# A two-layer decoder step on one core: first rows in a buffer of their own, decode rows kept in place, value products in pairs

## What is computed

```python
def trunk_layer(x, pos, conv_buf, shift_prev, rwkv_state, mem_k, mem_v, attend, p):
    h = rms_norm(x, p['pre_g'])
    proj = jnp.einsum('bsd,de->bse', h, p['w_in'])
    ...
    o_lat = attend(q_lat, q_rope, ckv, krope)
    ...
    x = x + rms_norm(jnp.einsum('bse,ed->bsd', mixed, p['w_out']), p['post_g'])

for l in range(DEPTH):                      # DEPTH = 2
    mk, mv = mem_kv(mem_prompt, mem_norm_g[l], w_mem_k[l], w_mem_v[l])
    xp, ... = trunk_layer(xp, pos_p, ..., mk, mv, prompt_attend, p)   # 2048 prompt rows
    xs, ... = trunk_layer(xs, pos_s, ..., cache_mem_k[l], cache_mem_v[l], ..., p)   # 8 decode rows
```

## Time and profile before

| | |
|---|---|
| median of 3 runs | 3659.76 us (3657.32 to 3660.7) |
| the profiled execution | 3655.21 us, its span 3653.4 us |
| TensorE busy, products | 3548.5 us, 97% of the span |
| TensorE, loads of weights (beside the products) | 2609.2 us, 71% |
| VectorE busy | 1693.9 us, 46% |
| ScalarE busy | 1385.9 us, 38% |
| GpSimd busy | 163.4 us, 4% |
| TensorE's granted clock, mean | 0.996 of full |
| moved by DMA | 411.45 MB, 113 GB/s |

### The profile page before, as it was taken

One profiled execution on the slowest core, in us unless ns is written; L12 is line 12 of the kernel. 1 busy time (PEld: TensorE's weight loads), 2 busy tenths in 40 slices (PEclk: granted clock), 3 DMA queues, 4 the chain that ended last, 5 costly groups with the idle time before them and its releaser, 6 DMA issues.

```text
span 3653.4 us, 74825 instructions
## 1 busy us (share of the span) xinstructions
PE 3548.5 (97%) x30920; PEld 2609.2 (71%) x30920; DVE 1693.9 (46%) x4364; ACT 1385.9 (38%) x3767; POOL 163.4 (4%) x284
## 2 busy tenths in 40 slices
PE   7999999999999999999989999999999999999998
PEld 5768686776768777686567686868777687776864
DVE  2535454454545535445325354544535454353553
ACT  2333434243343433534423333343433434335343
POOL 1000000000000000000000000000000000000000
PEclk9999999999999999999999999999999999999999
DMA  5343343425224143232343434334153241532411
GB/s 177 92 151 107 131 129 111 140 68 168 86 101 146 49 167 98 83 123 67 100 140 95 160 94 151 100 121 135 61 182 95 97 129 48 176 95 77 135 55 65
DMA packets 316661, 411.45 MB, mean 113 GB/s; under 512 B 26509, under 2 KB 276315, under 8 KB 316323
## 3 DMA queue, kind: packets, MB, share of 16 engines
q1 hardware_dynamic: 294243, 358.88, 30.5%
q0 software_dynamic: 11648, 41.95, 3.3%
q10 hardware_dynamic: 10432, 5.84, 0.6%
HBM read 384.84 MB, written 21.80 MB: 111 GB/s over the span
## 4 chain that ended last, share of the span: by engine, by line
PE 90%; ACT 5%; issue 2%; DVE 2%; ACTq 1%; DVEq 0%; DMA 0%; SPq 0%; POOL 0%; POOLq 0%
PE bank L714 82%; PE bank L718 8%; ACT hT L2141 1%; ACT Q L2301 1%; ACTq L2280 0%; ACT L2281 0%; ACT PT L2417 0%; ACT qr L2300 0%; DVEq L1393 0%; ACT Sm L2374 0%; ACT Q L2299 0%; DVE bon L1523 0%; ACT Bp L2322 0%; ACT T L2279 0%; ACT PT L2225 0%
## 5 line engine op out<-in xcount | busy, mean ns | idle before, releaser
L714 PE MATMUL bank<-hT,win 128*128 128x256 f32 (+3 forms) x7168 | 1607.5, 379 | 4.5 <-ACT hT L2141 4.5
L714 PEld LDWEIGHTS bank<-hT,win 128*128 128x128 f32 (+1 forms) x7168 | 1259.8, 186 | 222.4 <-issue 40.7
L714 PE MATMUL bank<-kv,Q 96*128 96x512 f32 (+3 forms) x640 | 276.5, 529 | 0.2
L1698 DVE TENSOR_REDUCE ml<-bank 128x1 f32<-128x512 f32 (+3 forms) x320 | 195.4, 611 | 158.8 <-PE bank L714 148.4
L718 PEld LDWEIGHTS bank<-cst,Sm 128*128 128x128 f32 x1344 | 153.5, 140 | 123.7 <-issue 67.6
L718 PE MATMUL bank<-cst,Sm 128*128 128x128 f32 x1344 | 213.7, 280 | 17.9 <-ACT Sm L2374 9.8
L2374 ACT ACTIVATE Sm<-bank,ml 128x512 f32<-128x512 f32 (+3 forms) x320 | 199.9, 625 | 74.4 <-DVE ml L1703 68.6
L714 PE MATMUL bank<-wout,mix 128*128 128x512 f32 x480 | 217.9, 600 | 6.8 <-ACT hT L2141 6.5
L2163 ACT ACTIVATE mix<-bank 128x256 f32<-128x256 f32 x128 | 49.0, 383 | 318.4 <-PE bank L714 318.4
L714 PEld LDWEIGHTS bank<-wout,mix 128*128 128x128 f32 x480 | 88.7, 191 | 113.1 <-issue 112.2
L2270 ACT ACTIVATE mix<-bank 128x512 f32<-128x512 f32 (+1 forms) x68 | 39.6, 596 | 250.2 <-PE bank L714 250.2
(11 more groups left out here) (480 smaller groups left out, 5691.2 us busy)
## 6 DMA issues: line engine op xcount, KB each, us to landing
win<-in_w_in SPq DMA_DIRECT2D x176, 1024.0 KB, 5.3
wout<-in_w_out SPq DMA_DIRECT2D x60, 512.0 KB, 7.7
out_xres<-xin SPq DMA_DIRECT2D x16, 1024.0 KB
xin<-in_x_prompt SPq DMA_DIRECT2D x15, 1024.0 KB
xin<-out_xres SPq DMA_DIRECT2D x15, 1024.0 KB
win<-in_w_in SPq DMA_DIRECT2D x16, 896.0 KB, 4.9
PT<-in_w_out SPq DMA_DIRECT2D x28, 512.0 KB, 3.6
XX<-in_w_out SPq DMA_DIRECT2D x28, 512.0 KB, 4.1
```

Of the source, the lines that this page charges most:

```text
L714: return pe.matmul(out, lhsT, rhs, start=start, stop=stop, skip_group_check=True)
L1698: v.tensor_reduce(top, bank[:, 0:w], AX, MAX)
```

## The change

Three things are changed.

1. The rows of block 0 get a buffer of their own, `xfirst`, in `kv[:, 4096:6144]`. SP loads it behind the memory weights (in layer 1 after a wait for the stored rows of block 0 of layer 0); ScalarE's load is gone. TensorE turns the first tile right behind the memory products, into banks 4 and 5, and ScalarE takes it and normalises the second tile before `memory_out`.
2. In layer 1 the decode rows are taken from `xin` as the residual left them. SP raises the count of `s_x` where it issued the load.
3. In the attention two value groups are issued together at every fourth chunk, in place of one at every second.

```diff
+        xfirst = kv[:, 4096:6144].rearrange("p (j d) -> p j d", j=2)
...
+        s_xf = sig("first_rows", 16)
...
# sync, memory_loads(l), at its end
+                if l:
+                    sp.wait_ge(s_od.h, s_od.at((l - 1) * IT + 1, 0))
+                sp.dma_start(xfirst, prompt_rows(l, 0)).then_inc(s_xf.h, 16)
...
                     sp.wait_ge(s_xn.h, s_xn.at(px, 0))
+                    if px == l * IT + 2:
+                        sp.sem_inc(s_x.h, 16)
                     sp.dma_start(xin[:, :, :], prompt_rows(l, tok)).then_inc(s_x.h, 16)
...
-                sp.dma_start(xin[0:NS, 0, :], sample_rows(l)).then_inc(s_x.h, 16)
+                    sp.dma_start(xin[0:NS, 0, :], sample_rows(l)).then_inc(s_x.h, 16)
+                else:
+                    sp.sem_inc(s_x.h, 16)
...
# tensor, attention
-                    if c >= m + 2 and (c - m) % 2 == 0:
+                    if c > m and (c - m) % 4 == 0:
+                        values((c - m) // 2 - 2)
                         values((c - m) // 2 - 1)
-                for x in range((n - m - 1) // 2, n // 2):
+                for x in range((n - m - 1) // 4 * 2, n // 2):
                     values(x)
...
# tensor, start of a layer, behind the memory products
                         turn_x(l * IT, 0, 2)
+                turn_x(l * IT + 1, 0, bank=4)
                 pe.wait_ge(s_mem["kvr"].h, s_mem["kvr"].at(l, 1))
...
-                pe.wait_ge(s_hT.h, s_hT.at(l * IT, 2))
-                turn_x(l * IT + 1, 0)
                 pe.wait_ge(s_wr.h, s_wr.at(l, 1))
                 turn_x(l * IT + 1, 1)
...
# scalar
+                def rows_of(px):
+                    return xfirst if px == l * IT + 1 else xin
...
-                    act.wait_ge(s_x.h, s_x.at(px, 16))
+                    if px == l * IT + 1:
+                        act.wait_ge(s_xf.h, s_xf.at(l, 16))
+                    else:
+                        act.wait_ge(s_x.h, s_x.at(px, 16))
...
                 act.wait_ge(s_xn.h, s_xn.at(px, 2))
-                act.dma_start(xin[:, :, :], prompt_rows(l, 0)).then_inc(s_x.h, 16)
                 sum_squares(px + 1, 2, junk)
                 act.wait_ge(s_xt.h, s_xt.at(px, 2))
                 normalise(px + 1, 0)
-                act.wait_ge(s_mem["kv"].h, s_mem["kv"].at(l, 2))
                 take_h(px, 0, slice(T, T + NS), 2)
+                take_h(px + 1, 0, tile_cols(0), bank=4)
+                normalise(px + 1, 1)
                 memory_out()
-                take_h(px + 1, 0, tile_cols(0))
-                normalise(px + 1, 1)
                 take_h(px + 1, 1, tile_cols(1))
```

More of the change, by code:

```diff
@@ L2125, in sum_squares @@
                             act.drain()
-                        act.activation(out[:, 0:D], xin[:, j, :], ACT.Square, accum_out=st[:, j:j + 1]).then_inc(s_ss.h, 2 // tiles)
+                        act.activation(out[:, 0:D], rows_of(px)[:, j, :], ACT.Square, accum_out=st[:, j:j + 1]).then_inc(s_ss.h, 2 // tiles)
                     act.drain()
@@ L2133, in normalise @@
                     act.wait_ge(s_xr.h, s_xr.at(px, j + k))
-                    act.mul(xn[:, :], xin[:, j, :], st[:, 4 + j:5 + j]).then_inc(s_xn.h, k)
+                    act.mul(xn[:, :], rows_of(px)[:, j, :], st[:, 4 + j:5 + j]).then_inc(s_xn.h, k)
                 def take_h(px, j, cols, k=1, bank=6):
```

## The result

| | kernel before | changed kernel |
|---|---|---|
| median, beside each other on one chip | 3659.52 us (3657.32 to 3660.7) | 3637.95 us (3634.6 to 3639.97) |
| profiled execution, its span | 3655.21, 3653.4 us | 3639.97, 3638.2 us |
| mean granted clock in it | 0.996 | 0.994 |

What follows compares the result with a forecast made beforehand. TensorE, busy 97% of the span, was taken as the bound. From 3655.2 us, 9.2 for the layer starts and 12.1 for pairing left 3633.9 for the profiled execution, 3638.5 for the median; range 3627 to 3650.

Steps and rivals of the forecast that it cites:

- Part 3: Attention: issuing value groups in pairs saves 12.1 us over both layers, the ceiling of 19.7 less added waits.
- the ceiling: Attention: 68 value groups no longer stand apart, each saving 0.29 us for going in and out, 19.7 us.
- The loss: Last five turns of a block: ScalarE paces bare turns, so waits take back part of the saving, 7.6 us.
- Rival A: Attention: pairing gives nothing, as the 0.29 falls on engines' waits everywhere; 3650.6 us, chance 0.09.
- rival D: Attention: doubled value groups starve the row maxima, TensorE waits at each of the 68; 3690.7 us, chance 0.05.
- Part 1: Start of layer 0: turning the first tile earlier brings the second turn 3.01 us forward, plus 0.26; sum 3.3 us.
- 0.26 more, with a shorter gap ahead of it: Start of layer 0: the second turn, 1.30 us before, runs at its full-clock 1.04, gaining 0.26 us.
- Rival C: Start of layer 0: the load put ahead on SP isn't hidden, and layer 0 starts later; 3645 us, chance 0.06.
- Part 2: Start of layer 1: 3.0 from the same order, 0.9 from the second turn, 1.95 from the dropped decode-row load; 5.9 us.
- the second turn should take 1.04: Start of layer 1: the second turn falls from 1.94 to 1.04 us, 0.9 gained.
- 1.2 of that wait remain: Start of layer 1: TensorE's wait of 3.11 us for the normalised decode rows shrinks to 1.2.
- Rivals B and E: B: ceiling reached and clock stays up, 3626.6 us, chance 0.08. E: clock alone, 4.3 less, 3634, chance 0.12.

Runs made afterwards that it cites:

- with the clock held: Kernels given transposes nobody reads in TensorE's waits: the kernel before took 3647.6 us, with both starts changed 3636.94, the changed kernel 3625.21.
- tail_filled: Changed kernel with paired value groups only while score products are still issued, single groups behind the last five turns of a block; 3633.06 us, ratio 0.9928.
- start_only: Changed kernel with the pairing of value groups undone, so only the layer starts are changed; 3649.06 us, ratio 0.9974.
- in_place_only: Kernel before with only the decode rows left in place in layer 1, not stored and loaded again; 3657.41 us, ratio 0.9999.
- warm_before: Kernel before with transposes nobody reads put into TensorE's waits, 28 in place of 11 ahead of the second turn; 3647.6 us.
- warm: `tail_filled` with 182 transposes of the identity, which nobody reads, ahead of or behind TensorE's waits in six places; 3618.84 us, ratio 0.9897.
- own_buffer_only: Changed kernel, but layer 1 stores and loads the decode rows again as before; 3642.72 us, ratio 0.9961.
- split_pairs: Changed kernel with the score product put between the two value groups of a pair; 3654.48 us, ratio 0.9992.

## Why the prediction was right, point by point

**Part 3, a forecast of 12.1: the size and the mechanism right, its two terms each too large.** 11.9 by the windows, 11.7 with the clock held. That a passage costs busy time, and that bare turns at a block's end take part of it back, is what the runs show. But the ceiling of 68 x 0.29 = 19.7 was in fact 16.7 of busy time, since the 0.29, read in mid-block, doesn't hold for all 68 (0.25 on average, and 0.09 for the groups that `tail_filled` sets apart again). The loss was counted at 7.6, and TensorE's idle time in these stretches rose by 4.8. Both errors are about 3 us and cancel, which is luck. In blocks 0 and 1 likewise: 0.43 and 0.87 came for 0.58 and 0.58, and most of it is waiting that went, not passages. The forecast used one number for two blocks; the two differ by up to 0.6, and the sum of each pair agrees to 0.2. The forecast of 2.86 us from score to turn was for 16 pairs of products; what stands there above has 14, for which the same terms give 2.64. Rival A (nothing, 3650.6) falls by that, and rival D (row maxima starved) since no turn in mid-block waits that did not before.

**Part 1, a forecast of 3.3 for layer 0: the position right, one term wrong.** Block 0 starts 3.58 us earlier (49.08 for 52.66). The total is close, two of its parts aren't. Ahead of the decode tile's turn (32.13 for 33.40) lie 1.27, mostly because the memory products happened to take 8.80 us for 9.93, where 7.03 is full clock. From there to the second turn are 2.99, forecast at 3.01. Behind it 0.68 were lost. The term "0.26 more, with a shorter gap ahead of it" failed: after a wait of 1.27, shorter than the 3.39 before, the turn took 1.97, not 1.04. With the clock held the moved turn is worth 2.98. Rival C falls: the decode tile's turn starts before 33.4. Its normalised rows are there at 28.75 (26.98 before), 1.8 us later and not 3.5, well inside the cover.

**Part 2, a forecast of 5.9 (3.0 + 0.9 + 1.95): 4.78 in the changed kernel, 5.66 in `start_only`.** By positions in the changed kernel the chain of the decode rows gave 1.82, for 1.95. From their turn to the second turn are 12.77 us for 15.76, so 2.99, for 3.0. From the second turn to block 0 are 4.24 for 4.21, so nothing, for 0.9. The step that failed is therefore "the second turn should take 1.04": it took 1.97, and only in `start_only`, where it took 1.09, did the 0.9 come (3.36). "1.2 of that wait remain" failed as well, but cost nothing. The wait stands behind the memory products, and these took 7.10 in the changed kernel and 8.80 before and in `start_only`: 1.70 faster and 1.70 more waiting, 3.00 in place of 1.30, with the turn 10.10 behind their start either way. `in_place_only` shows the same 1.8 alone and 1.3 of it lost to the clock before block 0, which fits a time that is that of the kernel before to within the noise.

**The clock: taken as unchanged.** In the profiled executions half clock cost 14.2 us of busy time in the changed kernel and 10.9 before, 3.3 more. In the medians there is no such loss: the change is worth 22.4 with the clock held (20.7 without the 1.7 that `warm_before` loses) and 21.6 as it is. Holding the clock gives the kernel before 9.6 us. It gives the changed one 12.7 by its median and 10.4 if that is corrected for the 2.3 us between the two medians of the kernel before. So on average the clock was about unchanged, as taken, with falls in other places. Block 0 starts at half clock as before. Rivals B and E, where less of the time is at half clock, fall. The Trainium skill (TensorE: Matmul & The Clock Gate, What's actually happening) says that activity releases the throttle. `warm` agrees, with a granted clock of 1.00; shorter waits alone, without work in them, did not do it (0.50 behind a wait of 1.27).

**The sum.** For an execution like the profiled one it said 3633.9, and this one took 3639.97. Of the 21.3 forecast, 20.3 are there by positions (11.9, 3.6 and 4.8). But 5.1 came back elsewhere, 1.0 in block 0's start, 1.7 near 210 us and 1.6 at the end, so this execution is only 15.2 us below the one of before. That the medians are 21.6 apart and the forecast was 21.3 is in part luck: they rest on four executions each, which spread over 3.4 and 5.4 us. With the clock held the agreement doesn't rest on that: 11.7 for the 12.1 of part 3, and 7.9 by positions (9.0 by medians) for the 9.2 of parts 1 and 2, of which 1.2 were clock.

Open: what decides the stretches at half clock near 210 and 3630 us. In the profiled executions without transposes in the waits, the first comes in all but the kernel before, `own_buffer_only` and `split_pairs`, the second in all but the kernel before and `split_pairs`. Open too: why a passage costs 0.30 to 0.34 us in mid-block and 0.09 in the groups of `tail_filled`.

## What to carry to other kernels

Look for what a busy engine loses between kinds of products: compare products side by side with the same products alone between others, multiply the difference by the number of changes, and group them where other work still hides the pace of the engine that feeds them; where it ends, go back to single ones. Measure the difference at each kind of place, since here it was 0.30 us or more in mid-block and 0.09 at the blocks' ends. A short wait removed at the start of a stage can be given back by the clock, so fill a wait of TensorE that can't be removed with products that nobody reads, and count them to end just before it does. Such a version is also the one in which small edits can be measured: its runs lie 0.6 to 2 us apart, those of the plain kernels 4 to 9. And read a small edit from positions in the timeline, not only from the total.

## What was not expected of the hardware

A turn of eight transposes ran at half clock, 1.97 us, behind a wait of only 1.27 in the changed kernel, and at full clock, 1.09, behind the same wait in `start_only` and behind one of 3.00 in the changed kernel. The length of the wait right before it doesn't decide. And 182 transposes whose results nobody reads made the kernel 14.2 us faster (`warm` against `tail_filled`).
